# Turning retention's gated outputs with VectorE and small SBUF copies instead of TensorE transposes

## What is computed

```python
o = retention(rq, rk, rv)                                   # 4 heads, value width 512
o = o * rsqrt(mean(o * o, axis=-1) + RMS_EPS)
o = o.reshape(B, S, RV_WIDTH) * ret_norm
ret_out = (silu(rg) * o) @ w_ret_out                        # 2048 x 2048
merged = g_pool * pool_out + g_attn * attn_out + g_ret * ret_out
```

## Time and profile before

| | us |
|---|---|
| median of three executions | 2449.19 (2449.02 to 2451.0) |
| the profiled execution | 2449.97 |
| its span | 2447.8 |
| PE busy | 2421.0, 99% |
| DVE busy | 1288.7, 53% |
| ACT busy | 1151.4, 47% |
| DMA engines, mean | some 60% busy, 192 GB/s |

### The profile page before, as it was taken

One profiled execution on the slowest core, in us unless ns is written; L12 is line 12 of the kernel. 1 busy time (PEld: TensorE's weight loads), 2 busy tenths in 40 slices (PEclk: granted clock), 3 DMA queues, 4 the chain that ended last, 5 costly groups with the idle time before them and its releaser, 6 DMA issues.

```text
span 2447.8 us, 32947 instructions
## 1 busy us (share of the span) xinstructions
PE 2421.0 (99%) x10824; PEld 2000.0 (82%) x10824; DVE 1288.7 (53%) x1405; ACT 1151.4 (47%) x1356; POOL 43.3 (2%) x50
## 2 busy tenths in 40 slices
PE   8999999999999999999999999999999999999998
PEld 6888888888887888888888888888788888888887
DVE  4555455554446555655555545555655455555444
ACT  5454454544445444444544444444554454544443
POOL 1000000000002000000000000000100000000000
PEclk9999999999999999999999999999999999999999
DMA  7566675666665555555666666655666576666664
GB/s 230 184 219 211 189 220 181 215 209 196 194 192 174 155 174 172 163 180 155 198 195 191 188 198 193 192 178 174 193 211 213 184 223 189 210 212 199 185 198 159
DMA packets 273118, 470.92 MB, mean 192 GB/s; under 512 B 23089, under 2 KB 67281, under 8 KB 272689
## 3 DMA queue, kind: packets, MB, share of 16 engines
q1 hardware_dynamic: 269376, 464.60, 61.2%
q0 software_dynamic: 1488, 5.68, 0.8%
q10 hardware_dynamic: 2208, 0.07, 0.1%
HBM read 456.64 MB, written 2.10 MB: 187 GB/s over the span
## 4 chain that ended last, share of the span: by engine, by line
PE 94%; SPq 2%; DVE 1%; DMA 1%; ACT 1%; issue 1%; DVEq 0%; ACTq 0%; POOL 0%; POOLq 0%
PE acc L563 30%; PE acc L565 30%; PE acc L564 30%; SPq L409 2%; PE bank L584 1%; ACT w_hi L897 1%; DMA w_raw<-in_ffn_up_dram 1%; DVE w_lo L1180 0%; PE bank L761 0%; PE bank L733 0%; DMA pre_gain<-in_ffn_pre_dram 0%; DVE xT_lo L1191 0%; DMA w_raw<-in_ffn_down_dram 0%; DVE hid_sb L1304 0%; PE bank L798 0%
## 5 line engine op out<-in xcount | busy, mean ns | idle before, releaser
L1180 DVE TENSOR_TENSOR w_lo<-w_raw,w_hi 128x1024 fp32r<-128x1024 f32 x856 | 1044.2, 1226 | 1065.3 <-ACT w_hi L897 1056.7
L897 ACT ACTIVATE w_hi<-w_raw 128x1024 fp32r<-128x1024 f32 x856 | 902.4, 1061 | 1195.4 <-PE acc L565 1026.4
L563 PE MATMUL acc<-w_hi,xT_hi 128*128 128x512 f32 x2464 | 969.5, 393 | 11.1 <-DVE w_lo L1180 6.8
L565 PE MATMUL acc<-w_hi,xT_lo 128*128 128x512 f32 x2464 | 961.1, 390 | 0.0
L564 PE MATMUL acc<-w_lo,xT_hi 128*128 128x512 f32 x2464 | 960.7, 390 | 0.0
L563 PEld LDWEIGHTS acc<-w_hi,xT_hi 128*128 128x128 f32 x2464 | 463.6, 188 | 113.4 <-DVE w_lo L1180 13.1
L565 PEld LDWEIGHTS acc<-w_hi,xT_lo 128*128 128x128 f32 x2464 | 463.5, 188 | 97.3
L564 PEld LDWEIGHTS acc<-w_lo,xT_hi 128*128 128x128 f32 x2464 | 463.9, 188 | 94.6 <-issue 1.0
L563 PE MATMUL acc<-w_hi,act_hi 128*128 128x512 f32 x704 | 274.3, 390 | 0.9 <-DVE w_lo L1180 0.9
L564 PE MATMUL acc<-w_lo,act_hi 128*128 128x512 f32 x704 | 274.0, 389 | 0.0
L565 PE MATMUL acc<-w_hi,act_lo 128*128 128x512 f32 x704 | 274.0, 389 | 0.0
(11 more groups left out here) (135 smaller groups left out, 943.0 us busy)
## 6 DMA issues: line engine op xcount, KB each, us to landing
w_raw<-in_ffn_up_dram SPq DMA_DIRECT2D x352, 512.0 KB, 4.4
w_raw<-in_ffn_down_dram SPq DMA_DIRECT2D x176, 512.0 KB, 4.7
w_raw<-in_w_gate_dram SPq DMA_DIRECT2D x96, 512.0 KB, 4.0
w_raw<-in_w_in_dram SPq DMA_DIRECT2D x72, 512.0 KB, 3.7
w_raw<-in_w_in_dram SPq DMA_DIRECT2D x128, 256.0 KB, 2.9
w_raw<-in_w_ret_out_dram SPq DMA_DIRECT2D x32, 512.0 KB, 4.7
w_raw<-in_w_out_dram SPq DMA_DIRECT2D x32, 512.0 KB, 4.5
hid_T<-blocks SPq DMA_DIRECT2D x352, 32.0 KB, 1.8
```

What stands on the lines that cost most here:

```text
L563: pe.matmul(pair[m][:, :], xh, wh, start=(first and kk == 0), stop=False)
L565: mm = pe.matmul(pair[m][:, :], xl, wh, start=False, stop=(last and kk == KG - 1))
L897: act.activation(w_hi[:, s, :], w_raw[:, s, :], ACT.Copy).then_inc(w_rounded, 1)
L1180: dve.tensor_tensor(w_lo[:, s, :], w_raw[:, s, :], w_hi[:, s, :].bitcast(f32), ALU.subtract).then_inc(w_split, 1)
```

## The change

`ret_transposes` is gone from PE, with the eight transposes per group, the claims on banks 0 and 1, and the branches around them. Instead:

- DVE, at the end of each heads iteration, waits for its own gated output and transposes 32x32 blocks of `gate_sb` into `ret_blocks`, which lies on `hid_sb`'s place (two instructions), and raises `ret_turned`.
- SP issues sixteen DMAs of 32 KB from `ret_blocks` to `ret_T` between the loads of groups 7 and 8 of the next iteration (or of `merge`'s first). `ret_T` lies on `gate_sb`'s place.
- `ret_hi` and `ret_lo` read `ret_T` in SBUF, behind group 5's round and rest instead of group 3's. `ret_lo` is now eight instructions of 128x128; `ret_hi` stays at four of 128x256.
- Since `ret_T` lies on `gate_sb`, ACT waits for `ret_split`, raised by the last of `ret_lo`, before it copies strip 0 into `gate_sb` behind `round_group(7)`; likewise in `merge`.

```diff
-SPLIT_PIECES = ("x0", "x1", "x2", "merged", "ret", "pool", "pv1", "pv0")
+SPLIT_PIECES = ("x0", "x1", "x2", "merged", "pool", "pv1", "pv0")
...
+        ret_blocks = sb("ret_blocks", [P, P // SQ, MT, 4, SQ], f32, at=tmp_at + 4 * MT * STRIP)
+        ret_T = sb("ret_T", [P, P // SQ, MT, 4, SQ], f32, at=tmp_at)
...
+            def turn_ret(g):
+
+                sp.wait_ge(ret_turned, g + 1)
+                for q in range(NQ):
+                    for to in range(NQ):
+                        sp.dma_start(ret_T[to * SQ:(to + 1) * SQ, q, :, :, :],
+                                     ret_blocks[q * SQ:(q + 1) * SQ, to, :, :, :]).then_inc(ret_landed, 16)
...
                 for n in range(4 * GD):
+                    if n == 2 * SLOTS:
+                        with sp.If(g > 0):
+                            turn_ret(before(g, KVH))
...
-            def ret_transposes(g):
-                pe.wait_ge(ret_ready, g + 1)
-                for half in range(2):
-                    claim("ret", half, g)
-                    for kk in range(2):
-                        for m in range(MT):
-                            k = 2 * half + kk
-                            last = transpose(bank[half][:, kk * SEQ + m * P:kk * SEQ + (m + 1) * P],
-                                             gate_sb[:, m, k * P:(k + 1) * P])
-                    last.then_inc(filled[half], 1)
...
             def ret_hi(g):
-                for half in range(2):
-                    wait_filled(act, "ret", half, g)
-                    for kk in range(2):
-                        k = g * 4 + (2 * half + kk)
-                        last = act.activation(retT_hi[:, ds(k, 1), :].rearrange("p a n -> p (a n)"),
-                                              bank[half][:, kk * SEQ:(kk + 1) * SEQ], ACT.Copy, scale=ret_gain[:, ds(k, 1)])
-                    last.then_inc(rounded[half], 1)
+                wait_ret(act, g)
+                for k in range(4):
+                    last = act.activation(ret_k(retT_hi, g * 4 + k), ret_tile(k), ACT.Copy, scale=ret_gain[:, ds(g * 4 + k, 1)])
+                last.then_inc(ret_rounded, 1)
...
+                    if n == SLOTS + 1:
                         with act.If(g > 0):
                             ret_hi(before(g, KVH))
                     if n == 7:
+                        act.wait_ge(ret_split, g + 1)
                         strip_out(g, n, 0, ACT.Copy)
...
             def ret_lo(g):
...
+                wait_ret(dve, g)
+                dve.wait_ge(ret_rounded, g + 1)
+                for k in range(4):
+                    for m in range(MT):
+                        at = ds(g * 4 + k, 1)
+                        last = dve.scalar_tensor_tensor(tokens(retT_lo[:, at, m * P:(m + 1) * P]), ret_T[:, :, m, k, :],
+                                                        ret_gain[:, at], tokens(retT_hi[:, at, m * P:(m + 1) * P]).bitcast(f32),
                                                         ALU.mult, ALU.subtract)
-                    last.then_inc(read[half], 1)
+                last.then_inc(ret_split, 1)
...
                 last.then_inc(ret_ready, 1)
+                dve.wait_ge(ret_ready, g + 1)
+                for m in range(MT):
+                    last = dve.transpose(ret_blocks[:, :, m, :, :].rearrange("p to k i -> p k to i"),
+                                         gate_sb[:, m, :].rearrange("p (k to j) -> p k to j", to=NQ, j=SQ))
+                last.then_inc(ret_turned, 1)
```

More of the change, by code:

```diff
@@ L93, in bank_uses @@
     for g in range(KVH):
-        if g:
-            use("ret", 0, 1)
         use("q", 0), use("window", 2)
@@ L263, in hybrid_trunk @@
         hid_split = sem("hid_split")
+        ret_turned = sem("ret_turned")
+        ret_landed = sem("ret_landed")
+        ret_rounded = sem("ret_rounded")
+        ret_split = sem("ret_split")
         def group(sec, i, n):
@@ L345, in wait_turned_in, with wait_ret, ret_tile, tokens @@
             eng.wait_ge(hid_landed, 16 * NQ * NQ * turns(f, p))
+        def wait_ret(eng, g):
+            eng.wait_ge(ret_landed, 16 * NQ * NQ * (g + 1))
+        def ret_tile(k):
+            return ret_T[:, :, :, k, :].rearrange("p q m i -> p m q i")
+        def tokens(a):
+            return a.rearrange("p a (q i) -> p (a q) i", i=SQ)
+        def ret_k(a, k):
+            return a[:, ds(k, 1), :].rearrange("p a (m q i) -> p (a m) q i", m=MT, i=SQ)
         def hid_tile(m):
@@ L461, in _ @@
                     for k in range(GD):
+                        if n == 2 * SLOTS:
+                            with sp.If(c < 1):
+                                turn_ret(KVH - 1)
                         load("merge", c, n, w_gate[k][:, :, ds(c * STRIP + br * D, STRIP)])
@@ L773, in _ @@
                             k_transposes()
-                        with pe.If(g > 0):
-                            ret_transposes(before(g, KVH))
                     if n == 8:
@@ L841, in _ @@
                         products("merge", c, n, xT_hi, xT_lo, KG * k, 2 * br, k == 0, k == GD - 1)
-                        if n == 3:
-                            with pe.If(c < 1):
-                                ret_transposes(KVH - 1)
                         n += 1
@@ L850, in _ @@
                     if br == 2:
-                        for b in range(2):
-                            wait_read(pe, "ret", b, KVH - 1)
+                        pe.wait_ge(ret_split, KVH + 1)
                     ng = GD if br == 2 else GH
@@ L1145, in _ @@
                         k = (7, 19, 31).index(n)
+                        act.wait_ge(ret_split, KVH + 1)
                         wait_strip(act, "merge", c, n)
@@ L1325, in _ @@
             dve.sem_inc(w_split, SLOTS)
+            dve.sem_inc(ret_split, 1)
             dve.memset(sq_post[:, :, :], 0.0).then_inc(sq_added, 1)
```

## The result

The changed kernel takes 2470.35 us (median of 6 runs, 2469.53 to 2472.19) beside 2449.32 (6 runs) for the kernel before: ratio 1.0086, 95% interval 1.0076 to 1.0097. That is 21.0 us more, where 9.0 were forecast; the direction was right and the time lies above the range. The profiled execution has a span of 2470.1, 22.3 more than before's.

What follows compares the result with a forecast made beforehand. PE, busy 99% of the span, was taken to bound the kernel. Three heads iterations at 2.7 us and merge at 0.9 sum to +9.0, the 3.5 gain included: 2449.2 + 9.0 = 2458.2 us, range 2452.5 to 2464.

Steps and rivals of the forecast that it cites:

- What bounds the kernel, and what goes: PE, busy 99% of the span; dropping eight transposes in each of four places gives 0.88 us each, 3.5 in all.
- SP's queue: From PE's iteration start T: copies at T+6.75 delay load 8 to T+17.1, its rounding on ACT to T+20.8.
- First wait: PE waits for late group 8 in each heads iteration with a turn: 1.4 us (1.1 to 3.1).
- It too is late: Group 9 also late; ACT's scalings start 2.25 us after t, the round of group 8, as in the SwiGLU.
- The rest of ACT and DVE's chain: ret_hi 1.55, ret_lo 2.1, strip 0's copy 1.25 us, ending at t+7.25, t being group 8's round on ACT.
- Second wait: PE, through group 8, waits 2.1 us before the queries' transposes for ACT's strip 0 copy, in three heads iterations.
- rival (c): PE's clock falls to its lower level behind waits, 1.6 us lost; one to three falls make 2460 to 2463; 17%.
- forecast loss of three iterations: Each of the three heads iterations with a turn loses 2.7 us, the transposes' gain included.
- Merge: One turn with 512 KB loads: PE starts group 8 at T+23.5, losing 0.9 us; no wait for strip 0's copy.
- (a): The turn is covered: SP issues sixteen copies in 6 us instead of 10.3; all 3.5 gained, 2445.7 us; 5%.
- (b): Only the wait at group 8 comes; queries late three times 0.6, merge 0.9: 2452.0 us; 11%.
- (d): Slow landings or ret_lo at 2.7 us add up to 1.7 and 0.6 an iteration: 2460 to 2465; 7%.

Runs made afterwards that it cites:

- e4_behind_11: Changed kernel with copies on SP's queue behind group 11's load instead of 7's, scalings behind group 13, ret_T on the score buffer: 2443.27 us, ratio 0.9988.
- e3_pool_queue: Changed kernel with the sixteen copies issued by POOL instead of SP: 2445.96 us, ratio 0.9998 to the kernel before.
- e9_hold: Kernel before, without copies; SP holds group 8's first half in every heads iteration until PE has used group 5: 2467.92 us beside 2447.2.
- e7_whole: Changed kernel loading strips 0 and 1 as one 512 KB DMA from neighbouring columns, computing with other columns of w_in: 2463.09 us, ratio 1.0061.
- e8_late_scale: Changed kernel with ret_T on the score buffer and, in heads alone, scalings behind group 13, copies left in place: 2462.9 us, ratio 1.0064.
- e6_after9: Changed kernel with SP holding group 10's load in each heads iteration until group 9 has landed: 2472.95 us, ratio 1.0111.
- e1_own_place: Changed kernel with ret_T on the idle score buffer, so strip 0 is copied without waiting for ret_split: 2466.4 us, ratio 1.0080.
- e5_sized_filler: Changed kernel with eight extra PE products in the wait before the queries' transposes, only in the three iterations with a turn: 2463.4 us, ratio 1.0068.

## Why the prediction was wrong, point by point

- **What bounds the kernel, and what goes.** Right. Eight transposes less in four places; `e4_behind_11`, where nothing else is disturbed, is 3.1 us faster than before (forecast of the gain: 3.5).
- **SP's queue.** Right to 0.1: copies at T + 6.75, load 8 at T + 17.1, round at T + 20.7 for a forecast of T + 20.8. `e3_pool_queue` shows that this queue is the cause: with the copies off it both waits but one of 0.6 are gone, and with them the 21 us.
- **First wait.** 1.17, 1.06 and 1.05 in heads for 1.4 (1.1 to 3.1), 1.41 in merge. Right, slightly high. The profile counts idle time from the end of the last product (0.39 long), while the forecast counted from when the next could start (0.23 behind its start); in the forecast's way each wait is 0.16 longer, the 1.17 is 1.33.
- **"It too is late": the step that failed.** The prediction moved group 9's round 1.29 behind group 8's and the scalings to t + 2.25, from a turn of the SwiGLU, where groups are whole 512 KB pieces. Here the round came 2.97, 2.27 and 3.21 behind t, so the scalings began at t + 3.9 (899.79 - 895.86). That alone moves the queries by 1.7, 1.0 and 1.9. Group 9's landing was never worked out from its own row: the earlier trace rows had a maximum of 4.8, and I took the median for the first load of a burst and silently for the others too. The second half of group 9 landed 4.7, 3.9 and 4.9 after its issue. `e9_hold` shows 2.8 to 3.15 for this burst without any turn, `e7_whole` 1.28 and 1.29 in two iterations for whole pieces, with group 10 late in one of them.
- **The rest of ACT and DVE's chain.** `ret_hi` 1.69 for 1.55, `ret_lo` 2.19 for 2.1, copy 1.27 for 1.25: from the scalings' start to the queries' transposes 5.64 (905.43 - 899.79) for a forecast of 5.05 (t + 2.25 to t + 7.3). Half of it is `ret_lo`'s start, 0.33 behind the end of `ret_hi` (901.81 - 901.48), for which 0.05 stood.
- **Second wait.** 4.19, 3.47 and 4.43 for 2.1: mechanism and place right, size half. Over three iterations 12.1 instead of 6.3, which is 5.8 of the 12 missing us. The two bullets above are its parts: 2.1 + 1.7 + 0.6 = 4.4, 2.1 + 1.0 + 0.6 = 3.7 and 2.1 + 1.9 + 0.6 = 4.6, each some 0.2 above the idle time in the profile, which is the 0.16 of counting.
- **The clock, rival (c).** It was given 17% and a price of 1.6 for each fall, from one wait of 1.92. It fell in all three iterations, at 2.3, 1.7 and 1.7, together 5.7, the other half of what is missing. The rival's condition was judged on waits of 1.4 and 2.1, and they were 1.1 and 3.5 to 4.4. Whether it would have stayed away with the forecast waits is not shown, and partly contradicted: in `e7_whole` the clock fell behind waits of 1.17 and 2.50, near the forecast ones, and held behind 1.20 and 3.40. So 17% looks too little even for the forecast waits, and that the waits were longer is not shown to be why. The Trainium skill, "TensorE: Matmul & The Clock Gate", section "HAM oscillation — how this bites in real kernels", tells of loops in which each wait for data brings the fall again; three of three iterations agree. Single iterations of `e7_whole`, `e8_late_scale` and `e9_hold`, with waits of 3.40, 2.40 and 2.58, do not.
- **What is left over.** The forecast loss of three iterations is 8.1, the second waits add 5.8, the clock 5.7, and the first waits take off 0.9: 18.7 of the 19.8 measured. The remaining 1.1 is no term of its own: six waits of 0.16 more by the forecast's way of counting are 1.0.
- **Merge.** 2.2 lost for 0.9. Besides 1.41 at group 8 (1227.33) PE waits 0.76 for a split at 1234.16, for group 9's round comes 3.06 behind group 8's there too (1224.96, 1228.02), though these pieces are whole.
- **Rivals (a), (b), (d).** The copies took 10.04, so (a) fell; the second wait came, so (b) fell. (d) named slow landings at 7% and 1.7 an iteration: this is what happened, in group 9 rather than 8, and together with (c) where each had been priced alone. The two were never added: (d)'s 3 x 2.3 and (c)'s 3 x 1.6 on 2458.2 make 2469.9. The range ended at 2464, below even the 2465 that (d) alone gave as its upper end.

**What stays open.** Why the second group of such a burst lands 2.3 to 3.2 behind the first. Half-width pieces are part of it (`e7_whole`), sharing with groups 10 and 11 a smaller one (`e6_after9`), but one iteration of `e7_whole` and merge show 2.5 to 3.1 with whole pieces, and in another of `e7_whole` group 10 was late instead. How the bank or row addresses of the source bear on it wasn't tried. Nor is it known what decides whether the clock falls behind a given wait.

## What to carry to other kernels

Small DMAs are paid in the queue that issues them, by whatever is queued behind: put them where that queue has work ahead for longer than they take (here behind load 11, or on an idle engine's queue) before asking what they carry. When a queue is freed late, work out every group of the burst behind it from the slow end of the landing row, not the first group alone, and follow them through the engine that stands in order behind them. Price a lengthened PE wait and the fall of the clock that may follow it as one case: it followed 16 of the 19 second waits of 2.4 to 5.5 us seen here, at 1.4 to 2.4 each.

## What the runs showed of the hardware

- A 32 KB SBUF-to-SBUF copy costs SP 0.63 us of its queue (10.04 for sixteen) and POOL 0.49 (7.86 for sixteen); from POOL the last has landed 11.9 after the first issue.
- In a burst of 256 KB loads (the changed kernel, g = 1) the first lands in 2.8, the third 4.6, the fifth 5.1 and the sixth 5.2 after its issue.
- PE's clock fell behind all nine second waits of 3.2 to 5.5 us in the changed kernel, `e1_own_place` and `e6_after9`, and behind seven of the ten in `e7_whole`, `e8_late_scale` and `e9_hold` (2.50 to 3.67); it held behind 2.40, 2.58 and 3.40, and behind the 0.7 left idle in `e5_sized_filler`. So the length of the wait alone does not tell. Two waits that the change leaves alone show the same: behind 1.8 at 745 us it held before and fell in the changed kernel, behind 1.9 at 1714 us (1737 in the changed kernel) it fell before and held after.
